# Gate projection interleaved with stick-breaking attention: its first weights loaded in the stage before, and its first products placed in attention's opening

## The reference

```python
proj = einsum('bsd,dp->bsp', rms(x), w_in)
o_a = rms(gated_delta_rule(q_a, k_a, v_a, g, beta), dn_out_gain) * silu(z_a)
o_b = stick_breaking(rms(q_b), rms(k_b), v_b) * silu(z_b)
# stick-breaking, for a block of 128 queries, keys up to its end, mask = key < query:
z = q @ k.T * d ** -0.5
log_keep = where(mask, log_sigmoid(-z), 0)
a = where(mask, exp(log_sigmoid(z) + sum of log_keep over later keys), 0)
out = a @ v
gates = sigmoid(proj[..., B_Z1:G1] + b_gate)          # 2 * 1024 channels
merged = gates[..., :D] * (o_a @ w_up_a) + gates[..., D:] * (o_b @ w_up_b)
x = x + merged @ w_out
```

## Time and the profile before

| what | value |
|---|---|
| median of three runs (lowest, highest) | 2705.22 us (2701.9, 2708.61) |
| the profiled execution, its own time | 2701.07 us |
| its span, first to last instruction | 2699.3 us |
| instructions | 37132 |
| PE busy | 2548.8 us, 94% |
| DVE, ACT, POOL busy | 54%, 37%, 13% |
| mean granted TensorE clock | 0.974 |

### The profile page before, as it was taken

The page is one execution under the profiler, slowest core; times in us unless marked ns, Lnnn a source line. Parts: engine busy times, 40 slices in busy tenths (PEclk is TensorE's granted clock), DMA queues, the critical chain, the costliest instruction groups (busy, mean ns, idle before and its releaser), DMA issues. The chain is left out here.

```text
span 2699.3 us, 37132 instructions
## 1 busy us (share of the span) xinstructions
PE 2548.8 (94%) x14438; PEld 2190.7 (81%) x14438; DVE 1456.7 (54%) x2148; ACT 999.4 (37%) x1721; POOL 354.4 (13%) x450
## 2 busy tenths in 40 slices
PE   7969999999599998999998898999899999999999
PEld 6849999999488887888887686878788888888887
DVE  6523444442366764534324776754787777733452
ACT  4223222221255664223213776752433333222331
POOL 1002222220233230001002323101000000000100
PEclk9989999999699998999999998999999999999999
DMA  4222122110333223442334211135322222255532
GB/s 143 87 84 84 52 63 69 50 44 30 106 120 104 83 63 136 164 164 93 104 103 143 68 38 44 58 118 175 74 98 75 86 86 94 70 193 182 180 113 82
DMA packets 215846, 264.76 MB, mean 98 GB/s; under 512 B 46932, under 2 KB 147924, under 8 KB 215672
## 3 DMA queue, kind: packets, MB, share of 16 engines
q1 hardware_dynamic: 215672, 262.38, 30.6%
HBM read 185.11 MB, written 77.22 MB: 97 GB/s over the span
## 5 line engine op out<-in xcount | busy, mean ns | idle before, releaser
L1379 PE MATMUL delta_acc<-delta_w_hi,xn_hi 128*128 128x256 f32 x640 | 190.9, 298 | 2.9 <-DVE delta_w_lo L1333 2.9
L1381 PE MATMUL delta_acc<-delta_w_hi,xn_lo 128*128 128x256 f32 x640 | 180.4, 282 | 0.0
L1380 PE MATMUL delta_acc<-delta_w_lo,xn_hi 128*128 128x256 f32 x640 | 180.3, 282 | 0.0
L4500 DVE TENSOR_TENSOR ffn_feed_lo<-ffn_feed_raw,ffn_feed_hi 128x1536 fp32r<-128x1536 f32 x44 | 77.4, 1759 | 143.7 <-ACT ffn_feed_hi L4491 143.7
L4200 PE MATMUL ffn_up_acc<-mixed_hi,ffn_ring_hi 128*128 128x512 f32 x348 | 135.6, 390 | 1.7 <-DVE ffn_gain_row L4120 1.3
L4200 PE MATMUL ffn_up_acc<-mixed_hi,ffn_ring_lo 128*128 128x512 f32 x348 | 135.4, 389 | 0.0
L4200 PE MATMUL ffn_up_acc<-mixed_lo,ffn_ring_hi 128*128 128x512 f32 x348 | 135.4, 389 | 0.0
L426 DVE TENSOR_TENSOR_SCAN stick_keep<-stick_keep,stick_zero 128x127 f32<-128x127 f32 (+7 forms) x64 | 92.4, 1443 | 74.2 <-ACT stick_keep L378 73.4
L1379 PEld LDWEIGHTS delta_acc<-delta_w_hi,xn_hi 128*128 128x128 f32 x640 | 121.4, 190 | 8.9 <-issue 5.5
L4491 ACT ACTIVATE ffn_feed_hi<-ffn_feed_raw 128x1536 fp32r<-128x1536 f32 x44 | 65.4, 1487 | 168.5 <-PE ffn_up_acc L4570 162.8
L1380 PEld LDWEIGHTS delta_acc<-delta_w_lo,xn_hi 128*128 128x128 f32 x640 | 121.4, 190 | 0.0
(11 more groups left out here) (494 smaller groups left out, 7120.9 us busy)
## 6 DMA issues: line engine op xcount, KB each, us to landing
ffn_feed_raw<-in_w_down SPq DMA_DIRECT2D x44, 512.0 KB, 4.0
ffn_ring_raw<-in_w_gate SPq DMA_DIRECT2D x11, 1024.0 KB, 5.3
ffn_ring_raw<-in_w_up SPq DMA_DIRECT2D x11, 1024.0 KB, 5.3
scratch_act_t<-ffn_silu SPq DMA_DIRECT2D x22, 512.0 KB, 3.2
ffn_feed_raw<-scratch_act_t SPq DMA_DIRECT2D x44, 256.0 KB, 2.9
delta_w_raw<-in_w_in SPq DMA_DIRECT2D x20, 512.0 KB, 4.0
scratch_projected<-delta_out SPq DMA_DIRECT2D x80, 128.0 KB, 1.7
stick_g_raw<-in_w_in SPq DMA_DIRECT2D x16, 512.0 KB, 4.5
```

The costliest lines, as they stand in the source:

```text
L1379: nc.tensor.matmul(acc, self.hi[:, k, tok], w_hi, start=(k == 0), stop=False, skip_group_check=True)
L1380: nc.tensor.matmul(acc, self.hi[:, k, tok], w_lo, start=False, stop=False, skip_group_check=True)
L1381: last = nc.tensor.matmul(acc, self.lo[:, k, tok], w_hi, start=False, stop=(k == self.kt - 1), skip_group_check=True)
L4500: self.nc.vector.tensor_tensor(self.lo[s][:], self.raw[s][:], self.hi[s][:].bitcast(F32), ALU.subtract).then_inc(self.lo_done[s], 1)
```

## The change

1. A new stage `EarlyGate` joins the delta phase. It has SP instructions only: it waits for an event early in the delta rule and issues the loads of gate weight tiles 0 and 1 and of the bias. It stands in the plan 40 entries ahead of the end. The tiles lie at the end of SBUF, where the stick phase takes them over; the gate's low parts are written over them as before.
2. Stick's generators yield inside their opening: x of tile 0, squares, sums, inverse and scales are step s1, turns 0 and 1 are s2, turns 2 and 3 are s3, the squares, sums and scales of tile 1 are s4.
3. The gate's generators yield once ahead of their first half product (g1: the splits of tile 0 on ACT and DVE, nothing on PE and SP).
4. The plan `stick_plan` begins g1, s1, g2, g3, s2, g4, s3, g5, s4, g6, g7, and then takes the 68 steps with the other 59 gate steps spread over them. Steps i = 0, 7, 15, 22, 30, 37, 45, 52 and 60 have none.

```diff
+SBUF_END = 229344
@@ StickAttention.sync (the other engines alike)
         self.prep.load(sp, 0)
         self.prep.load_gains(sp)
+        yield
         sp.dma_start(self.v_sb[:], self.v.rearrange("(k p) d -> p k d", p=P)).then_inc(self.v_in, 16)
+        yield
         self.prep.load(sp, 1)
+        yield
+        yield
@@ StickAttention.scalar
         self.prep.squares(act, 0)
+        yield
         act.wait_ge(self.prep.gain_scaled, 1)
         for s in QUARTERS:
             self.prep.keep_hi(act, 0, s)
+            if s % 2:
+                yield
         self.prep.squares(act, 1)
+        yield
@@ StickAttention.tensor
+        yield
         for s in QUARTERS:
             prep.turn(pe, 0, s)
+            if s % 2:
+                yield
+        yield
@@
+class EarlyGate:
+    SIZE = 2 * 4 * D + 64
...
+    def sync(self, sp):
+        self.delta.pre.wait(sp, "exps", 4)
+        for i in range(2):
+            sp.dma_start(self.raw[i][:], self.source(i).rearrange("(k p) n -> p k n", p=P)).then_inc(self.loaded[i], 16)
+        with self.nc.allow_non_contiguous_dma(reason="one bias a channel"):
+            sp.dma_start(self.bias_sb[:], self.bias.rearrange("(i p) -> p i", p=P)).then_inc(self.bias_in, 16)
+        yield
@@ GateProjection.sync
-        load(0)
-        with self.nc.allow_non_contiguous_dma(reason="one bias a channel"):
-            sp.dma_start(self.bias_sb[:], self.bias.rearrange("(i p) -> p i", p=P)).then_inc(self.bias_in, 16)
-        load(1)
         for i, half, part in self.walk():
+            if i == 0 and half == 0 and part == 0:
+                yield
@@ GateProjection.tensor
+        yield
@@
-def even_plan(first, second):
-    plan, given = [], 0
-    for i in range(first):
-        plan += [0, 2]
-        want = second * (i + 1) // first
-        plan += [1] * (want - given)
+def stick_plan(steps, others):
+    stick, gate, branches = range(3)
+    plan = [gate, stick, gate, gate, stick, gate, stick, gate, stick, gate, gate]
+    given = first = plan.count(gate)
+    for i in range(steps):
+        plan += [stick, branches]
+        want = first + (others - first) * (i + 1) // steps
+        plan += [gate] * (want - given)
         given = want
     return plan
@@ two_blocks
+                run_stages(ph, [DeltaFront(delta), DeltaBack(delta), DeltaScan(delta), tokens, early_gate],
+                           plan[:-40] + [4] + plan[-40:])
```

More of the change, by code:

```diff
@@ L354, in gpsimd @@
         self.nc.gpsimd.memset(self.zero[:], 0.0).then_inc(self.zeroed, 1)
-        for j in range(2):
-            self.prep.inverses(pool, j)
+        self.prep.inverses(pool, 0)
+        yield
+        yield
+        yield
+        self.prep.inverses(pool, 1)
+        yield
         for i in range(self.steps()):
@@ L493, in tensor, with __init__, sems, takes @@
             yield
+class EarlyGate:
+    SIZE = 2 * 4 * D + 64
+    def __init__(self, nc, at, kt, source, bias, delta):
+        self.nc, self.kt, self.at, self.source, self.bias, self.delta = nc, kt, at, source, bias, delta
+        self.tiles = bias.shape[0] // P
+        self.raw = [nc.alloc_sbuf_tensor_at(f"early_g_raw{s}", [P, kt, P], F32, offset=at + 4 * kt * P * s) for s in range(2)]
+        self.bias_sb = nc.alloc_sbuf_tensor_at("early_g_bias", [P, self.tiles], F32, offset=at + 8 * kt * P)
+        self.loaded, self.bias_in = [nc.alloc_semaphore(f"early_g_loaded{s}") for s in range(2)], nc.alloc_semaphore("early_g_bias")
+    def sems(self):
+        return self.loaded + [self.bias_in]
+    def takes(self, at):
+        return []
+    def sync(self, sp):
[4 more added lines that the diff above has]
+            sp.dma_start(self.bias_sb[:], self.bias.rearrange("(i p) -> p i", p=P)).then_inc(self.bias_in, 16)
+        yield
+    def gpsimd(self, pool):
+        return iter(())
+    def scalar(self, act):
+        return iter(())
+    def vector(self, dve):
+        return iter(())
+    def tensor(self, pe):
+        return iter(())
@@ L496, with __init__ @@
 class GateProjection:
-    def __init__(self, ph, nc, hi, lo, kt, source, bias, out):
-        self.nc, self.hi, self.lo, self.kt, self.source, self.bias, self.out = nc, hi, lo, kt, source, bias, out
+    def __init__(self, ph, nc, hi, lo, kt, source, early, out):
+        self.nc, self.hi, self.lo, self.kt, self.source, self.out = nc, hi, lo, kt, source, out
         self.tiles = out.shape[0] // P
         self.w_hi = [ph.sb(f"g_hi{s}", [P, kt, P], F32R) for s in range(2)]
[L504 to L508, removed]
+        self.w_lo = [nc.alloc_sbuf_tensor_at(f"stick_g_lo{s}", [P, kt, P], F32R, offset=early.at + 4 * kt * P * s) for s in range(2)]
+        self.raw, self.bias_sb = early.raw, early.bias_sb
@@ L509, in __init__ @@
         self.gate = [ph.sb(f"gate{b}", [P, HALF]) for b in range(2)]
         self.acc = ph.ps("g_acc", [P, HALF])
-        self.loaded = ph.sem2("g_loaded")
-        self.hi_done, self.lo_done, self.bias_in, self.summed, self.gated = (
-            ph.sem(f"g_{n}") for n in ("hi_done", "lo_done", "bias_in", "summed", "gated"))
+        self.loaded, self.bias_in = early.loaded, early.bias_in
+        self.hi_done, self.lo_done, self.summed, self.gated = (ph.sem(f"g_{n}") for n in ("hi_done", "lo_done", "summed", "gated"))
@@ L514, in __init__ @@
         self.stored = ph.sem2("g_stored")
     def steps(self):
-        return 4 * self.tiles + 1
+        return 4 * self.tiles + 2
     def walk(self):
@@ L4943, in two_blocks @@
                                          lambda i, m: rest[m * P:(m + 1) * P, i * W:(i + 1) * W])
-                run_stages(ph, [DeltaFront(delta), DeltaBack(delta), DeltaScan(delta), tokens], delta_plan(tokens.steps()))
+                gate_source = lambda i: w_in[:, gate_col + i * P:gate_col + (i + 1) * P]
+                early_gate = EarlyGate(nc, SBUF_END - EarlyGate.SIZE, 8, gate_source, a["b_gate"], delta)
+                assert nc.sbuf_base <= early_gate.at
+                plan = delta_plan(tokens.steps())
+                run_stages(ph, [DeltaFront(delta), DeltaBack(delta), DeltaScan(delta), tokens, early_gate],
+                           plan[:-40] + [4] + plan[-40:])
             with Phase(nc, "stick") as ph:
@@ L4947, in two_blocks @@
                                        gated[:, HALF:D], c)
-                gate = GateProjection(ph, nc, hi, lo, 8, lambda i: w_in[:, gate_col + i * P:gate_col + (i + 1) * P], a["b_gate"],
-                                      gates)
+                ph.sems += early_gate.sems()
+                gate = GateProjection(ph, nc, hi, lo, 8, gate_source, early_gate, gates)
                 branch_gates = BranchGates(ph, nc, stick, o_a, z_a, qkv_z_b[:, 1536:], a["dn_out_gain"], gated)
-                run_stages(ph, [stick, gate, branch_gates], even_plan(stick.steps(), gate.steps()))
+                assert nc.sbuf_base <= early_gate.at
+                run_stages(ph, [stick, gate, branch_gates], stick_plan(stick.steps(), gate.steps()))
         x1, z2 = scratch("x1", SEQ, D), scratch("z2", SEQ, 1952)
```

## The result

The changed kernel takes 2691.52 us (median of five, 2685.65 to 2694.51) against 2706.68 us (five, 2701.90 to 2708.84). The ratio is 0.9943 with a 95% interval of 0.9924 to 0.9961: 15.2 us less, where 17 were forecast. Its profiled execution took 2685.65 us, 15.4 less than that of before.

The account below looks back on a forecast made before the run. PE was taken to bound the stick phase behind its opening, a chain of other engines the opening. 6.4 + 17.4 - 5.7 - 0.6 = 17.5 us, less 0.5 for the clock, gave 2688.2 us from 2705.2; range 2681 to 2698.

Parts of the forecast that it names:

- Early loads, cost 0: Delta phase: SP issues the gate's two weight loads and bias inside its own wait at about 630 us, costing nothing.
- g1 to g3: Start of the opening: PE starts at 687.8 us and ends the first two half products at about 696, or 698.3.
- The step on the table load: ACT in the opening: the sigmoid's 1.28 us table load runs right behind tile 0's squares, from 689.8 us, and is free.
- By turns: Opening: g5's sigmoid delays tile 1's turn by 3.6 us, yet flip(0) comes at 721.6 us, a 6.4 us gain.
- Half products out of the bound stage: Behind flip(0): six half products fewer for PE at 2.90 us each, a gain of 17.4 us.
- the emptied steps: Steps 7 and 15 (h = 7): PE waits 2.9 us each for DVE's scales, giving back 5.7 us.
- a fall in the opening's gap: Opening, from 712.2 to 714.4 us: PE's clock may fall while it is idle; 0.5 us taken off the gain.
- copies at 0.2 us: Empty steps with h = 4 to 6: each costs a 0.2 us wait for a copy, 0.6 us in all.
- No wait behind emptied steps: Rival, dense stage: PE finds the turns ready or wins elsewhere; gain 23 us, 2682 us; chance 0.14.
- Low clock through the whole opening: Rival, opening: PE's clock stays low from 697.5 us on; gain only 7 us, 2698 us; chance 0.17.
- Slower by the clock: Rival: the low clock lasts past the opening into the dense part; up to 10 us slower, 2715 us; chance 0.04.
- Early loads that hold up the delta phase: Rival, delta phase: token stores are delayed and PE waits for output buffers; gain 7 to 12 us; chance 0.05.

Follow-up runs that it names:

- the repeat: The changed kernel run once more with no edit: ratio 0.9945 to the kernel before, stage 360.2 us.
- empty steps moved: Changed kernel with the two empty steps at i = 7 and 15 (h = 7) put at i = 5 and 13: ratio 0.9922 to the kernel before.
- squares first: Changed kernel with tile 1's squares, sums and scales (s4) put ahead of g5: ratio 0.9933 to the kernel before.
- six empty steps: Changed kernel with empty steps i = 22, 30, 37, 45 put at 23, 31, 39, 47 (h = 7): ratio 1.0012 to the kernel before.
- loads only: Changed kernel keeping the early loads, but with the opening and three empty steps of the kernel before: ratio 0.9991 to that kernel.
- front only: Changed kernel with only the first two half products in the opening and five empty steps, none at h = 7: ratio 0.9933 to the kernel before.
- all three edits: Changed kernel with s4 and the branches' first step ahead of g5, and empty steps off h = 7: 2677.83 us, 0.9894 of the kernel before.

## Why the prediction was right, step by step

- **Early loads, cost 0.** Shown: SP's queue takes them in 2.6 us inside its own wait. That the loads by themselves are worth little was not a step of the prediction, but it wrote "what is removed is SP's gate loads and the 8.1 us wait"; the run of the loads alone gave 2.1 us, and the wait stayed at 6.55. The rest of the stage's 15.9 us came with the new place of the splits and the half products.
- **g1 to g3.** PE began 2.4 us into the stage, as worked out, the clock rose 5 us later, and the products ended ahead of turn 0. The step on the table load was wrong: it did not run behind the squares but behind the wait for the products (695.23, after 6.37 us of idle time), unlike in the earlier trace rows. Why is open. The load took 1.28 us and its ACTIVATE began 0.02 us behind it, so no drain stood between. It cost nothing that matters, since the sigmoid ended at 697.22 and the first keep_hi began at 697.48.
- **By turns.** 6.4 us forecast, 6.8 measured (6.0 in the repeat, with its low stretch). The squares held up by g5's sigmoid (3.6 forecast, 2.9 measured) and flip(0) held up by branch a's load are both shown, and each was undone by its own edit.
- **Half products out of the bound stage, less the emptied steps.** 11.1 us forecast, 9.1 measured. The two waits at h = 7 were 2.96 and 2.71 us against 2.9 each; with the empty steps moved off h = 7 one of 1.2 us is left, and with four more empty steps there four more waits come.
- **The terms that were mis-sized** are the clock and the half product. The prediction took 0.5 us for a fall in the opening's gap and none behind the emptied steps. In the profiled execution there was none in the gap and one behind step 7, which cost 1.5 us (4.42 - 2.90); in the repeat there were both. The second term is the 2.90 us for each half product: it is the time from a half product's first matmul to PE's next row, but taking one out of the dense part makes PE's busy time less by only 2.7 us. The rest of the kernel before, against that with the empty steps moved, which has no low clock there either and six half products less:

```profile
728.15:1056.30 328.15, 324.60 (x1968) 281.55 (x1967) 209.14 (x193) 183.85 (x322) 92.31 (x63) 1.00 0.28 86
```

```profile
721.23:1034.65 313.42, 308.52 (x1895) 268.31 (x1895) 208.87 (x193) 179.39 (x316) 95.23 (x68) 1.00 0.28 85
```

That is 16.1 us less of PE work, where 17.4 were forecast: 1.3 of the missing 2.0 us. (The run with only two half products in the opening gives the same price, 10.9 us for four.) The clock is 1.4 more (PE busy 309.9 us in the changed kernel against 308.5), and 0.3 comes behind the last matmul. Against this PE's idle time grew by 5.3 us and not by 6.3. So the hit on the sum owes something to errors that cancel.
- **A slip in the count.** The prediction charged copies at 0.2 us for "five against two" empty steps outside h = 7; from its own lists the steps with h = 4 to 6 are six (22, 30, 37, 45, 52, 60) against two, 0.8 us and not 0.6. The waits for copies measured 0.3 us against 0.2 before, so the charge was too high in either form.
- **The rivals.** No wait behind emptied steps: out, by the 5.7 us. Low clock through the whole opening: out, it was high from 8 us on. Slower by the clock: out in this kernel. Early loads that hold up the delta phase: out, SP's first load of attention's x came at 684.61 us instead of 685.39, and between 683.45 and 686.27 us in the seven other profiles with the early loads. As a mechanism, though, the clock can take part of the gain back, and waits the rest: with six waits in the dense stage instead of two, the kernel was as slow as before the change (1.0012), and its stage 4.9 us longer.

## What to carry to other kernels

A filler that is moved out of an engine-bound stage leaves holes; look what each hole stood in front of. Here one kind of step in eight needed all 2.9 us of its filler as cover, and choosing which steps stay empty was worth 5 us at no cost. Put a load or a small operation that others wait for ahead of the filler, not behind it, on every engine whose order the filler shares: a wait of ACT for PE's filler, and an SP queue that waits for scales before it issues another stage's load, were worth 1.8 and 2.5 us of the opening. And count a PE wait of near 3 us in a dense stage at more than its length: here four more of them took 10.8 us as idle time and 9.8 through the clock.

## What was not expected of the hardware

- Short waits of PE in an otherwise dense stage went with the lower clock, with some regularity. The wait of 2.9 to 3.0 us at step 7 had a low stretch behind it or from within it in all four executions that had this wait (changed, again, squares first, six empty steps). So had the waits of steps 23, 31, 39 and 47 in the kernel with six (2.8 to 2.9 us), and the 2.53 us ahead of flip(0) with the squares first. But the wait ahead of flip(0) in the kernel with six, 2.62 us, had none, nor had the 2.26 us in the changed kernel, and the wait of 2.7 us at step 15 had none in any of the four. A low stretch could begin when PE was already busy again: from 743 us, after PE had resumed at 741.8. In the rest of the stage of the kernels whose waits there were all 1.6 us or less (before, empty steps moved, loads only, front only, all three edits) there was none. Why step 15 and the waits ahead of flip(0) differ is open: the length of a wait doesn't decide it by itself.
- The same gap of 1.85 us ahead of tile 1's turn was followed by a low stretch in one execution of the changed kernel and not in the other, with the same instructions. It was also followed by one with the empty steps moved, but 1.95 us in the kernel with six empty steps at h = 7 was not.
- A table load on ACT ran ahead of its ACTIVATE's wait in one place and behind the wait in another (695.23).
